# Spreading the layer zero modulation steps of a fused two-block transformer over every second weight block

## The chip, the cores and the metric

The kernel runs on one core of one Trainium2 chip. The metric is device time in microseconds (us). The kernel before takes 2114.54 us, the median of 3 runs (2113.99 to 2114.84).

The engines are called PE (TensorE), DVE (VectorE), ACT (ScalarE), POOL (GpSimd) and SP (SyncE, which issues the DMAs).

## The reference

Two stacks of two layers each run on 256 tokens of width 1024. The first stack is modulated by a condition vector `c`; only it matters here. Cut to what matters:

```python
c_act = jax.nn.silu(c)
for l in range(2):
    mod = c_act @ w_ada[l] + b_ada[l]                  # 6 x 1024 numbers
    sh1, sc1, gt1, sh2, sc2, gt2 = jnp.split(mod, 6, axis=-1)
    h = modulate(rms_norm(x, norm_mix[l]), sh1, sc1)
    p = h @ w_in[l]
    y_att  = dilated_mixture_attention(...)            # from p
    y_rwkv = rwkv7_time_mix(...)                       # from p, a scan over the tokens
    y_gmlp = chunked_spatial_gating(...)               # from p
    ys = jnp.stack([y_att, y_rwkv, y_gmlp], axis=2)
    gates = jax.nn.sigmoid(p[..., i2:])
    merged = jnp.sum(gates * (ys @ w_branch[l]), axis=2)
    x = x + gt1 * (merged @ w_out[l])
    h = modulate(rms_norm(x, norm_ffn[l]), sh2, sc2)
    x = x + gt2 * conv_gated_ffn(h, ...)
```

The second stack (`second_block`: gated feed-forward, windowed attention beside a convolution, feed-forward, a per-layer embedding) needs no modulation.

## The kernel before

Activations stay on chip, features on the partitions. All large weights come as one stream of 664 blocks of eight 128 x 128 tiles (512 KB a block), in the order in which PE uses them. A block is loaded into one of seven buffers `raw`, ACT rounds it into one of five buffers `hi`, and DVE subtracts (`lo = raw - hi`, line 214 in the profile). PE then multiplies with both halves for accuracy.

The modulation is computed beside this, on DVE alone: for each of the 48 columns of 128 numbers of a layer, a 128 x 1024 block of `w_ada` is loaded into one of two buffers `ada` (512 KB by DMA) and one DVE instruction multiplies it with the row `crow` and sums (line 231). It is followed by a short read of the accumulator into `mod`. This pair is called a modulation step. Sixteen of layer 0's are done at the start of the program; the other 32, and then the 48 of layer 1, are spread through what follows.

What sets the order is `ORDER`, a list that `main_order` writes out by hand and that each of the five engines' programs walks through, and a `Flow` object in each of them. `Flow.tiles(n)` counts weight tiles; after each block (8 tiles) it calls the block's own work and then `tick`, which advances every side chain by one step: the recurrent scan (`rwkv`), attention, and `ada`, the modulation. On DVE the block's own work at the end of block b is the `lo` of block b+4. On ACT it is the `hi` of block b+5, and on SP the load of block b+7. SP's side step is the load of the `ada` block two further on, which waits until DVE has done the modulation step of this tick, since it takes over its buffer. All DMAs of SP are issued in the order of its program.

How often `ada` takes a step:

```python
def ada_order(f, step):
    for l in range(L):
        for m in range(0 if l else FIRST, 48):
            while f.pause:
                yield
            step(l, m)
            if m % 8 == 7:
                f.mods.add((l, m // 8))
            yield
            if l or m >= 40:
                yield
            if f.slow:
                yield
```

So a layer 0 column below 40 takes a step at every block unless `slow` is set, and the rest at every second block, or every third under `slow`. `("pause", ...)` items stop it; `("pause if", (l, 4))` stops it only if group 4 (columns 32 to 39) of that layer is already done; `("need", l, g)` catches up at once if group g is not.

The items of a layer, with the blocks of layer 0 (layer 1's are 148 further on): the `z` projections and `gmlp` (up to block 26, modulation paused), `gate`, `qk`, `v`, `branch2` (to 46), `gate` again (to 54), `branch0`, `branch1` and `merge` (54 to 70), `wout` (70 to 78), `norm2` (to 80), `up` (80 to 124), `down` (124 to 146). Names used later: `var_t` and `rs_t` hold the two gates in turn that `branch0` multiplies; `mg` holds the merged branches in two halves, made by the four `merge` items on ACT (high half) and DVE (low half), and read by PE in `wout`; `xT` is the residual stream, which DVE updates after each of the eight `wout` results, and whose squares PE sums in `norm2` before the second norm; `pfh` and `pfl` are operands of a small projection (`p_proj`) that PE does around `norm2`.

In `wout` the first two results are summed together, over k from 0 to 7, so PE needs the last quarter of `mg` (k = 6, 7) 12 tiles after its start.

Of the kernel before, what the change touches and what calls it, by code (L numbers as in the profile page):

```python
# [375 lines left out]
def main_order():  # L376

    s = []
    for l in range(L):
        s += [("start1", l), ("z first", l)] if l else [("pause", True), ("start",)]  # L380
        for p in (6, 2, 3, 0, 1, 4, 5):
            s += [("z", l, p), ("flag", ("z", l, p))]
            if p == (3 if l else 0):
                s += [("rwkv", l), ("pause", True)]
        if l == 0:
            s += [("bias table",)]
        s += [("gmlp v", l), ("token norm", l), ("gmlp u", l, 0), ("gmlp u", l, 1), ("gate", l, 2, 0),
              ("until", ("ln", l)), ("spatial", l), ("gate", l, 2, 1), ("gmlp y", l), ("flag", ("gmlp", l)),
              ("pause", False), ("gate", l, 2, 2), ("gate", l, 2, 3), ("until", ("prep", l))]
        s += [("qk", l, p) for p in range(4)] + [("v", l), ("attention1", l)]  # L390
        s += [("branch2", l, p) for p in range(4)] + [("flag", ("ys free", l)), ("until", ("qk free", l))]
        s += [("gate", l, 1, p) for p in range(4)] + [("finish", ("att1", l))]
        s += [("branch0", l, 0), ("branch0", l, 1), ("branch0", l, 2), ("finish", ("rwkv", l)), ("pause if", (l, 4))]
        s += [("branch0", l, 3), ("pause if", (l, 4)), ("branch1", l, 0), ("merge", l, 0), ("branch0", l, 4), ("branch1", l, 1), ("branch0", l, 5),
              ("merge", l, 1), ("branch0", l, 6), ("branch1", l, 2), ("branch0", l, 7), ("merge", l, 2), ("branch1", l, 3)]
        s += [("need", l, 2), ("out half", l), ("merge", l, 3), ("pause if", (l, 4))]
        s += [("wout", l, p) for p in range(4)] + [("need", l, 3), ("need", l, 4), ("norm2", l), ("slow", True)]
        s += [("up first", l)] + [("up", l, m) for m in range(KF + 2)] + [("down", l, p) for p in range(4)]
    for l in range(L):
        s += [("f first", 1, l)] + [("f", 1, l, m) for m in range(KF + 2)] + [("f down", 1, l, p) for p in range(4)]  # L400
        s += [("mixer2", l), ("c", l, 0), ("c", l, 1), ("c", l, 2), ("conv2", l), ("c", l, 3), ("c last", l)]
        s += [("qkv", l, 0), ("qkv", l, 1), ("taps", l, 0), ("qkv", l, 2), ("v2", l), ("taps", l, 2), ("qk norm", l), ("attention2", l)]
        s += [("gate2", l, 0), ("v2 turn", l)] + [("gate2", l, p) for p in range(1, 8)] + [("gate2 last", l), ("finish", ("att2", l))]
        s += [("attn out", l, 0), ("attn out", l, 1), ("attn out", l, 2), ("finish", ("conv2", l)), ("conv out", l, 0),
              ("attn out", l, 3), ("conv out", l, 1), ("conv out", l, 2), ("conv out", l, 3)] + [("wo", l, p) for p in range(4)]
        s += [("f first", 2, l)] + [("f", 2, l, m) for m in range(KF + 2)] + [("f down", 2, l, p) for p in range(4)]
        s += [("ple", l, m) for m in range(8)]
    return s


ORDER = main_order()
MAIN, WIDE, GEN, ONE, STAT = (0, 1, 3), (0, 1, 4, 5, 6, 7), (4, 5, 6, 7), (2,), (3,)
CONV, ATT2 = (4,), (5, 6, 7, 2)
# [2620 lines left out]
```

How the kernel before makes its waits and increments, by code:

```python
    def wait_ge(self, sig, name=None):  # L190
        if name is None:
            v = sig.n
        else:
            assert self.e is None or name in sig.at, name
            v = sig.at.get(name, 0)
        if v > self.seen.get(id(sig), 0):
            self.seen[id(sig)] = v
            if self.e is not None:
                self.e.wait_ge(sig.handle, v)
# [429 lines left out]
            def take(pool, use):  # L629
                before = ps.take(pool, use)
                if before in ps.freed:
                    pe.wait_ge(*ps.freed[before])
                return ps(use)
# [3 lines left out]
            def tile(keys):  # L637
                b, i = divmod(f.n, BT)
                n = len(keys)
                assert i + n <= BT
                if e is None:
                    order.extend(keys)
                pe.wait_ge(v_main, ("lo", b))
                f.n += n
                cols = slice(i * 128, (i + n) * 128)
                return hi[b % HL][:, cols], lo[b % RAW][:, cols], [("block", b)] if i + n == BT else []
# [1 line left out]
            def plain_tile(key):  # L649
                b, i = divmod(f.n, BT)
                if e is None:
                    order.append(key)
                pe.wait_ge(d_raw[b % RAW], ("raw", b))
                f.n += 1
                return raw[b % RAW][:, i * 128:(i + 1) * 128], [("block", b)] if i == BT - 1 else []
# [17 lines left out]
            def h_in(norm):  # L674
                return (lambda k: t256(hh, k), lambda k: t256(hl, k), lambda k: pe.wait_ge(v_main, ("h", norm, k)))
```

## Time and profile before

| | |
|---|---|
| median of the runs | 2114.54 us |
| profiled execution, own time | 2114.51 us |
| span of its trace | 2112.7 us |
| PE busy | 2091.4 us, 99% |
| PE weight load busy | 1900.4 us, 90% |
| DVE busy | 1641.4 us, 78% |
| ACT busy | 1232.7 us, 58% |
| DMA queue of SP | 422.08 MB, 59.2% of 16 engines |

Busy shares are over the whole span. Matmuls are pipelined: a row gives a matmul of 256 columns some 0.28 us, while the next starts 0.12 us after it. The span is 1.8 us short of the execution's own time, which agrees with the median.

### The profile page before, as it was taken

What the parts mean: (1) busy time and instruction counts of PE and PEld (TensorE: products, weight loads), DVE (VectorE), ACT (ScalarE), POOL (GpSimd) and SP (SyncE); (2) the same over time, 40 slices, a digit from 0 to 9 for tenths busy, and PEclk for the clock granted to TensorE, in tenths of its full rate; (3) what the DMA queues carried; (4) which work ended last, traced back from release to release, by engine and by line L of the source; (5) the groups of instructions that cost most, each with busy time, mean ns of one, the idle gap of its engine ahead of it and who ended that gap; (6) DMA issues with size and microseconds to landing.
All of it is one profiled execution on the core that took longest, in us unless ns stands there. A gap on an engine that the chain in (4) does not pass through costs nothing.

```text
span 2112.7 us, 39171 instructions
## 1 busy us (share of the span) xinstructions
PE 2091.4 (99%) x16342; PEld 1900.4 (90%) x16342; DVE 1641.4 (78%) x2528; ACT 1232.7 (58%) x1999; POOL 13.1 (1%) x20
## 2 busy tenths in 40 slices
PE   8999999999999999999999999999999999999999
PEld 6888999999998899998888989888898888998888
DVE  7899788888887788877887657787688765788876
ACT  4754756555755656555665448665475644766554
POOL 0000000000000000000000000000000000000000
PEclk9999999999999999999999999999999999999999
DMA  9566567768644467655555654555555557356553
GB/s 372 199 212 211 178 218 256 244 225 289 225 157 170 165 210 235 212 187 189 184 191 187 231 159 155 203 190 189 189 181 189 190 196 221 134 178 208 190 189 131
DMA packets 122115, 424.59 MB, mean 201 GB/s; under 512 B 13465, under 2 KB 22041, under 8 KB 121170
## 3 DMA queue, kind: packets, MB, share of 16 engines
q1 hardware_dynamic: 121938, 422.08, 59.2%
q8 instruction: 129, 2.11, 0.4%
q14 instruction: 48, 0.39, 0.1%
HBM read 417.68 MB, written 4.35 MB: 200 GB/s over the span
## 4 chain that ended last, share of the span: by engine, by line
PE 88%; DVE 6%; ACT 4%; DMA 1%; issue 1%; POOL 0%; SPq 0%; ACTq 0%; DVEq 0%
PE bank L208 88%; ACT arena L259 2%; DVE arena L214 2%; DVE lo L214 2%; ACT hi L259 1%; DVE arena L222 1%; DMA raw<-W 1%; PE bank L211 0%; DVE sml L234 0%; DVE ada L231 0%; DMA xT<-x 0%; ACT L251 0%; DVE arena L218 0%; ACT L259 0%; DVE arena L237 0%
## 5 line engine op out<-in xcount | busy, mean ns | idle before, releaser
L208 PE MATMUL bank<-h,hi 128*128 128x256 f32 (+1 forms) x5248 | 1183.1, 312 | 0.0
L259 ACT ACTIVATE hi<-raw 128x1024 fp32r<-128x1024 f32 x656 | 689.1, 1057 | 530.8 <-PE bank L208 458.6
L208 PE MATMUL bank<-h,lo 128*128 128x256 f32 x3328 | 949.1, 285 | 1.4 <-ACT arena L259 1.2
L208 PEld LDWEIGHTS bank<-h,hi 128*128 128x128 f32 x5248 | 861.4, 190 | 60.3 <-issue 1.9
L214 DVE TENSOR_TENSOR lo<-raw,hi 128x1024 fp32r<-128x1024 f32 x656 | 791.8, 1220 | 96.0 <-ACT hi L259 95.1
L208 PEld LDWEIGHTS bank<-h,lo 128*128 128x128 f32 x3328 | 633.7, 190 | 13.3 <-issue 7.8
L208 PE MATMUL bank<-act,hi 128*128 128x512 f32 x1056 | 370.0, 393 | 0.0
L208 PE MATMUL bank<-act,lo 128*128 128x256 f32 x1056 | 294.7, 279 | 0.0
L208 PEld LDWEIGHTS bank<-act,hi 128*128 128x128 f32 x1056 | 197.9, 187 | 47.1
L208 PEld LDWEIGHTS bank<-act,lo 128*128 128x128 f32 x1056 | 197.9, 187 | 0.0
L259 ACT ACTIVATE arena<-arena 128x256 f32<-128x256 f32 (+4 forms) x202 | 98.5, 493 | 159.2 <-DVE arena L214 151.4
L259 ACT ACTIVATE arena<-bank 128x256 f32<-128x256 f32 (+3 forms) x419 | 170.5, 449 | 23.5 <-PE bank L208 22.0
L208 PE MATMUL bank<-arena 64*64 64x64 f32 (+8 forms) x2940 | 144.7, 281 | 5.0 <-DVE arena L222 2.2
L214 DVE TENSOR_TENSOR arena<-arena 128x256 f32<-128x256 f32 (+2 forms) x237 | 123.8, 527 | 22.0 <-ACT arena L259 17.9
L208 PEld LDWEIGHTS bank<-arena 64*64 64x64 f32 (+4 forms) x2940 | 105.9, 137 | 35.0 <-DVE arena L222 4.0
L214 DVE TENSOR_TENSOR act<-arena,act 128x256 fp32r<-128x256 f32 x132 | 56.0, 424 | 79.1 <-ACT act L259 78.6
L231 DVE CUSTOM_DVE_ANT_0 ada<-ada,crow,par 128x1024 f32<-128x1024 f32 x80 | 104.3, 1303 | 0.2
L222 DVE SCALAR_TENSOR_TENSOR arena<-arena,par 128x256 f32<-128x256 f32 (+1 forms) x124 | 60.5, 503 | 23.8 <-ACT arena L259 20.6
L214 DVE TENSOR_TENSOR arena<-bank,arena 128x256 f32<-128x256 f32 (+2 forms) x182 | 69.3, 424 | 3.4 <-ACT arena L259 3.4
L222 DVE SCALAR_TENSOR_TENSOR xT<-bank,xT 128x256 f32<-128x256 f32 x96 | 40.6, 422 | 35.1 <-PE bank L208 33.5
L259 ACT ACTIVATE act<-arena 128x256 fp32r<-128x256 f32 x132 | 52.9, 401 | 4.8 <-DVE arena L214 4.8
L208 PE MATMUL bank<-ysh,lo 128*128 128x256 f32 x192 | 55.0, 287 | 0.0
(153 smaller groups left out, 1943.6 us busy)
## 6 DMA issues: line engine op xcount, KB each, us to landing
raw<-W SPq DMA_DIRECT2D x664, 512.0 KB, 3.4
ada<-WA SPq DMA_DIRECT2D x80, 512.0 KB, 3.9
arena<-WA SPq DMA_DIRECT2D x16, 512.0 KB, 14.2
arena<-conv_rows SPq DMA_DIRECT2D x16, 280.0 KB, 5.9
arena<-taps SPq DMA_DIRECT2D x2, 1792.0 KB, 8.4
p_projected<-arena SPq DMA_DIRECT2D x2, 1024.0 KB, 7.6
arena<-p_projected SPq DMA_DIRECT2D x2, 1024.0 KB, 4.8
arena<-scr SPq DMA_DIRECT2D x10, 128.0 KB, 4.5
```

The costliest lines, as they stand in the source:

```text
L208: return self.done(lambda e: e.matmul(out, l, r, start=start, stop=stop, skip_group_check=True))
L214: return self.done(lambda e: e.tensor_tensor(out, a, b, op))
L222: return self.done(lambda e: e.scalar_tensor_tensor(out=out, in0=a, scalar=s, in1=b, op0=o0, op1=o1))
L231: return self.done(lambda e: e.tensor_tensor_reduce(out, a, b, 1.0, start, MUL, ADD, total))
L259: return self.done(lambda e: e.activation(out, in_, f, scale=scale, **kw))
```

## The change

One item is added to layer 0's list. `("slow", True)` stands right behind `("pause", False)`, after `gmlp y`. Layer 1's list is unchanged.

```diff
         s += [("gmlp v", l), ("token norm", l), ("gmlp u", l, 0), ("gmlp u", l, 1), ("gate", l, 2, 0),
               ("until", ("ln", l)), ("spatial", l), ("gate", l, 2, 1), ("gmlp y", l), ("flag", ("gmlp", l)),
-              ("pause", False), ("gate", l, 2, 2), ("gate", l, 2, 3), ("until", ("prep", l))]
+              ("pause", False)] + [("slow", True)] * (1 - l) + [("gate", l, 2, 2), ("gate", l, 2, 3), ("until", ("prep", l))]
```

`slow` is set back at layer 1's start, as before. Counting blocks through `ORDER` gives where the steps stand (number of blocks finished when the step is taken):

| | before | now |
|---|---|---|
| layer 0, blocks 27 to 50 | 24 steps, one at every block | 12 steps, one at every second |
| layer 0, 51 to 57 | 4 steps | 4 steps |
| layer 0, 59 to 69 (`branch0`, `merge`) | none | 6 steps |
| layer 0, 71 to 78 (`wout`) | none | 4 steps: 71, 73, 75, 78 |
| layer 0, `norm2` to `down` (79 to 145) | 23 steps, every third block | 22 steps, every third block, shifted (81 to 144) |
| layer 1, 147 to 207 | 21 steps | 21 steps |
| layer 1, 209 to 217 (`branch1`, `merge`) | none | 5 steps |
| layer 1, `up` | 8 steps, to 248 | 6 steps, to 242 |

The reason for the new places: in layer 0, group 4 was complete at block 50, and both `pause if` items at blocks 58 and 70 stopped the chain. Now it is complete at block 73. In layer 1 it was complete at 207 and is now at 213.

PE's, ACT's and POOL's instructions keep their order. DVE's and SP's change. In the order of DVE's instructions the numbers of buffers are kept (`lo_61` to `lo_67` are the seven buffers, so one row is one block).

DVE in the branch stage of layer 0, around blocks 63 to 65, as the difference of the order (`arena<-arena,bank` is the gated branch of a `branch1`, the rows on `var_t` are a `branch0`):

```order
 L214 TENSOR_TENSOR lo_64<-raw_52,hi_57 128x1024
+L231 ISA ada_68,mod<-ada_68,crow,par 128x1024
+L231 ISA mod 128x1
 L222 SCALAR_TENSOR_TENSOR arena<-arena,bank 128x512
 L214 TENSOR_TENSOR arena<-arena 128x512
 L214 TENSOR_TENSOR lo_65<-raw_53,hi_58 128x1024
 L214 TENSOR_TENSOR lo_66<-raw_54,hi_59 128x1024
+L231 ISA ada_69,mod<-ada_69,crow,par 128x1024
+L231 ISA mod 128x1
 L222 SCALAR_TENSOR_TENSOR var_t<-var_t,bank 128x256
 L214 TENSOR_TENSOR arena<-arena,var_t 128x256
```

A step is put in behind every second `lo`, ahead of the branch arithmetic of that block. Six of them stand in this stage.

DVE at the end of layer 0's `wout`, where the last result (`xT`, two instructions) is added and the gain of the second norm (`sml<-mod,par`) is formed:

```order
 L214 TENSOR_TENSOR lo_65<-raw_53,hi_57 128x1024
+L231 ISA ada_69,mod<-ada_69,crow,par 128x1024
+L231 ISA mod 128x1
 L222 SCALAR_TENSOR_TENSOR xT<-bank,sml,xT 128x256 x2
 L222 SCALAR_TENSOR_TENSOR sml<-mod,par 128x8
```

The step of block 78 stands between the last `lo` and the last update of `xT`. The step that stood inside the norm (block 79) is gone.

## Rows read from the trace of the kernel before

**Rows 1.** The page's part 1, busy time and instructions of each engine

```profile
PE 2091.4 (99%) x16342; PEld 1900.4 (90%) x16342; DVE 1641.4 (78%) x2528; ACT 1232.7 (58%) x1999; POOL 13.1 (1%) x20
```

**Rows 2.** Part 5: groups, busy us, mean ns, idle before; then part 6, issues

```profile
L214 DVE TENSOR_TENSOR lo<-raw,hi 128x1024 fp32r<-128x1024 f32 x656 | 791.8, 1220 | 96.0 <-ACT hi L259 95.1
...
L231 DVE CUSTOM_DVE_ANT_0 ada<-ada,crow,par 128x1024 f32<-128x1024 f32 x80 | 104.3, 1303 | 0.2
...
raw<-W SPq DMA_DIRECT2D x664, 512.0 KB, 3.4
```

**Rows 3.** Waits of PE, 128 to 160, 190 to 194, 194 to 200 us

```profile
PE bank L208 <- ACT arena L259: 0.3, 1, 0.3
...
PE bank L208 <- DVE arena L222: 1.4, 2, 1.1
...
PE bank L208 <- DVE arena L222: 0.2, 1, 0.2
```

**Rows 4.** Chain that ended last: start us, us, what; both layers' scans

```profile
189.29 1.19 DVE ada L231
...
193.63 5.33 PE bank L208 x72
...
221.54 1.46 PE bank L211 x12
...
682.50 5.33 PE bank L208 x72
...
710.41 1.46 PE bank L211 x12
```

**Rows 5.** Windows: stretch, its us, busy us by engine, PEclk, DMA, GB/s

```profile
260.00:292.00 32.00, 32.00 (x269) 32.00 (x269) 27.66 (x39) 17.20 (x24) 0.00 (x0) 1.00 0.60 208
292.00:315.00 23.00, 23.00 (x134) 20.07 (x134) 20.55 (x35) 13.23 (x18) 0.00 (x0) 1.00 0.62 201
```

**Rows 6.** Timeline of DVE, layer 0 branches: start, us, instruction, idle before

```profile
262.19 1.28 DVE L231 CUSTOM_DVE_ANT_0 ada<-ada,crow,par 128x1024 f32<-128x1024 f32 x1
263.40 0.08 DVE L231 DVE_READ_ACCUMULATOR2_ANT mod<- 128x1 f32 x1
...
269.71 0.42 DVE L222 SCALAR_TENSOR_TENSOR var_t<-var_t,bank 128x256 f32<-128x256 f32 x1 [1.25 <-ACT var_t L259]
...
291.28 0.42 DVE L222 SCALAR_TENSOR_TENSOR var_t<-var_t,bank 128x256 f32<-128x256 f32 x1 [1.92 <-ACT var_t L259]
...
296.00 0.69 DVE L214 TENSOR_TENSOR mg<-arena,mg 128x512 fp32r<-128x512 f32 x1 [0.69 <-ACT mg L259]
```

**Rows 7.** Timeline of PE in layer 0's `wout`

```profile
296.40 0.28 PE L208 MATMUL bank<-mg,lo 128*128 128x256 f32 x1
...
296.74 0.39 PE L208 MATMUL bank<-mg,lo 128*128 128x256 f32 x1
```

**Rows 8.** Timeline, `wout` and `norm2` of layer 0, DVE, PE and ACT

```profile
298.30 1.23 DVE L214 TENSOR_TENSOR lo<-raw,hi 128x1024 fp32r<-128x1024 f32 x1 [0.47 <-ACT hi L259]
...
316.00 1.00 DVE L222 SCALAR_TENSOR_TENSOR xT<-bank,sml,xT 128x256 f32<-128x256 f32 x2
...
316.48 1.73 PE L208 MATMUL bank<-arena,cst 128*128 128x256 f32 x6
...
317.04 0.42 ACT L259 ACTIVATE arena<-xT 128x256 f32<-128x256 f32 x1 [0.67 <-DVE xT L222]
```

**Rows 9.** Timeline of DVE, layer 1's branches

```profile
771.52 0.42 DVE L222 SCALAR_TENSOR_TENSOR var_t<-var_t,bank 128x256 f32<-128x256 f32 x1 [0.75 <-ACT var_t L259]
...
774.83 0.42 DVE L222 SCALAR_TENSOR_TENSOR rs_t<-rs_t,bank 128x256 f32<-128x256 f32 x1 [0.69 <-ACT rs_t L259]
...
777.29 0.69 DVE L222 SCALAR_TENSOR_TENSOR arena<-arena,bank 128x512 f32<-128x512 f32 x1 [0.45 <-PE bank L208]
...
783.03 0.42 DVE L222 SCALAR_TENSOR_TENSOR var_t<-var_t,bank 128x256 f32<-128x256 f32 x1 [1.92 <-ACT var_t L259]
...
787.74 0.69 DVE L214 TENSOR_TENSOR mg<-arena,mg 128x512 fp32r<-128x512 f32 x1 [0.69 <-ACT mg L259]
```

## The prediction

> **What bounds the kernel now.** I read the busy times first. PE is busy for 99% of the span and DVE for 78% [rows 1]. So PE looks like the bound, and a change that only moves DVE work can act in one way alone: where PE waits for DVE, or would come to. The work itself does not change: 80 modulation steps before and after, and 656 `lo` of some 1.2 us each, one a block [rows 2]. A step keeps DVE for 1.21 us: it starts at 262.19, and the accumulator read, with the next instruction beside it, starts at 263.40 [rows 6].
>
> Next, the waits of PE in the stage that is relieved, blocks 27 to 50 or 120 to 225 us. DVE is nearly full there, and one might take it for the bound. But PE's waits add up to little: 0.3 us for ACT before 160 us, 1.4 us for DVE near 192 us in two waits, and 0.2 us in 194 to 200 [rows 3]. From 200 to 260 us the same view has one more of 0.2 us, near 200, which is the same wait cut by the window.
>
> The chain shows why. Shortly before 193.63 it runs through DVE, modulation steps included. Then it is on PE. And it can be compared with layer 1, which takes a step only at every second block already. The same scan work lasts from 193.63 to 221.54 in layer 0 and from 682.50 to 710.41 in layer 1: 27.91 us in both [rows 4]. In these 28 us a step at every block costs PE nothing against one at every second.
>
> Last, the stage that receives the steps. In `branch0`, `branch1` and `merge` of layer 0 (260 to 292 us) PE is busy for all of the 32 us and DVE for 27.66; in `wout` (292 to 315 us) DVE is busy for 20.55 of 23 [rows 5]. So there is idle time of 4.3 and 2.5 us. What counts is where it lies, and what hangs on DVE's last instruction of each stage.
>
> **The change part by part.**
>
> 1. *Twelve steps leave blocks 27 to 50.* That is 12 x 1.21 = 14.5 us of DVE time. What PE can gain is bounded by its waits, 0.3 + 1.4 + 0.2 = 1.9 us [rows 3]. One of the two waits near 192 and the small ones also occur in stretches of layer 1 at the slower rate. I take 1.4 us, of the bounds 0 and 1.9: the steps at blocks 40, 42 and 44 go, which frees 3.6 us just before the largest wait.
>
> 2. *Six steps enter layer 0's branch stage (blocks 59 to 69).* 6 x 1.21 = 7.3 us. DVE waits there for the gates from ACT, 1.25 us at 269.71 and 1.92 us at 291.28, and these waits absorb steps [rows 6]; the first takes in one step of 1.21, the last 1.92. The other idle times, of some 0.7 us before an `mg`, are answers of ACT to DVE's own result (0.69 at 296.00), so they move with it. Thus the low half of the last `mg` comes 7.3 - 1.2 - 1.9 = 4.1 us later, where all else holds. PE needs it at once: it is written from 296.00 to 296.69, and the matmul that reads it starts at 296.74, where a row of this form lasts 0.39 us in place of 0.28, so PE has already waited 0.1 us [rows 6, 7]. Nothing covers this: `wout` is PE's next work and its other k are done. Cost 4.1 us, with bounds 0 and 7.3 (six steps, nothing absorbed). The `lo` blocks run ahead, so they stay covered: the wait of PE would begin only if DVE lagged by more than about three blocks.
>
> 3. *Four steps enter `wout` (71, 73, 75, 78).* 4 x 1.21 = 4.8 us. The 4.1 us of part 2 moved PE and DVE alike, so this counts anew. One idle time of 0.47 us absorbs [rows 8]. From `pfl` at 302.35 us on DVE works without a break to the last `xT` at 316.00, and PE is just in time again: it starts the sums of squares at 316.48, and the last of their operands is the square that ACT forms from 317.04 to 317.46, while six matmul records fill 316.48 to 317.85 [rows 8]. All of the norm follows behind. So PE gets 4.8 - 0.5 = 4.3 us more to wait, 4.4 with rounding on the side of the `pfl` chain, which goes through ACT. Bounds 1.2 (the step of block 78 alone, which stands between the last `lo` and the last `xT`) and 4.8. The step in the norm at block 79 goes, but PE has the rest of `p_proj` to do meanwhile, and I count nothing for it.
>
> 4. *Five steps enter layer 1's branch stage (209 to 217), none its `wout`.* 5 x 1.21 = 6.0 us. DVE idles more there behind the first of them: 0.75, 0.69, 0.45 and 1.92 us [rows 9], 3.8 us in all. The last `mg` at 787.74 is as tight for PE as in layer 0. Cost 6.0 - 3.8 = 2.2 us, bounds 0 and 6.0.
>
> 5. *The steps in `up` and `down` shift by one block or two, and layer 1's `up` loses two.* No wait of PE stands there. Counted at nothing; the cover is that PE's `lo` are three blocks ahead, and if that were gone one step would cost 1.2 us.
>
> 6. *SP.* The 512 KB loads move with the steps. SP waits with a load until the step of the same tick is done, and weights queue behind it. A weight block lands 3.4 us after its issue [rows 2], and is issued seven blocks of 2.9 us ahead, so a delay of some 6 us is still covered. Counted at nothing, bounds 0 and one block, 2.9 us.
>
> Sum: -1.4 + 4.1 + 4.4 + 2.2 = +9.3 us. The profiled execution took 2114.51 us itself (span 2112.7 and 1.8 around it), which is the median of the runs (2114.54) within 0.03. So 2114.5 + 9.3 = 2123.8 us.
>
> A rule stands against this sum. The Trainium skill, in Perfetto Trace Analysis, "Identifying the Most-Contended Engine", says that the engine with the highest occupancy is the most contended one, that DVE's occupancy can be read as its distance from roofline, and that for TensorE the share of weight loads is to be read in place of matmul time. By that, DVE with 78% has room, PE with weight loads of 90% decides, and steps moved on DVE would change nothing: 2114.5. The rule's mechanism here is the first rival.
>
> **The rivals.**
>
> *No change, from 2110.3 to 2118.7.* DVE's lag is taken up by slack that I don't see. For it: PE shows no wait in 260 to 330 us, and DVE had 4.3 us of idle time in a stage that gets 7.3. Against it: the two places where PE is within 0.1 us of DVE [rows 7, 8]. It needs the `mg` chain of both layers to be hidden; then the norm's 4.4 less 1.4 gives 2117.5.
>
> *Faster.* The relieved stage gives more than its waits show, since DVE there runs late by a block and more, and the late stages absorb the steps. The mechanism: twelve steps less let PE start each matrix step of the scan earlier, at up to 1.21 us each. It decides if more than 9.3 us of the 14.5 came back, or if parts 2 to 4 are covered. At full cover of those and the whole of rows 3 it gives 2114.5 - 1.9 = 2112.6, so to pass 2110.3 it needs over 4 us from the scan. The equal 27.91 us of both layers speaks against it [rows 4].
>
> *Much slower, over 2127.* The loads decide. The weights behind a step's load are late, ACT rounds late, and DVE waits for ACT on top of its own lag: about one block, 2.9 us, in layer 0's branch stage, so 2126.7, and more if `wout` has it too.
>
> **How the numbers follow.** The forecast, with at least two of parts 2 to 4 at about their size, has 0.74. No change 0.12, much slower 0.10, faster 0.04. A measurement here tells 0.2%, or 4.2 us, from no change. So faster has 0.04, same 0.12, and slower the rest, 0.84. The range goes from 2117.0 (the norm alone, a little hidden) to 2127.5 (parts 2 to 4 and one late block).
>
> **What the profile after would show.** If part 2 is right, DVE has no idle time before the `var_t` that stood at 291.28, and PE waits some 4 us in the first two blocks of layer 0's `wout`, for `mg` (L214, from DVE). If part 3 is, PE waits 4 us more right behind `wout`, for the squares of `xT`, on ACT or DVE. If part 4 is, a wait of 2 us stands at the same place of layer 1, and none at its norm beyond what was there. If part 1 is, the wait near 192 us shrinks from 1.4 to some 0.3 us, and the blocks around it last the same. The forecast is wrong if PE's waits for DVE in `wout` are under 1 us, if the stretch from 120 to 225 us gets shorter by over 3 us, or if waits for raw weights show up.

## The result and the profile after

| | before | after |
|---|---|---|
| median of the runs | 2114.55 us (4 runs, 2113.99 to 2114.84) | 2125.69 us (4 runs, 2123.51 to 2126.32) |
| profiled execution, own time | 2114.51 us | 2126.32 us |
| span of its trace | 2112.7 us | 2124.2 us |

After divided by before is 1.0051, 95% interval [1.0038, 1.0063]. The forecast was 2123.8 us in a range of 2117.0 to 2127.5. So the kernel became slower by 11.1 us where 9.3 were forecast.

First the busy times of the page after, part 1 and one group of part 5, which answer to [rows 1, 2]:

```profile
PE 2096.0 (99%) x16342; PEld 1904.0 (90%) x16342; DVE 1641.0 (77%) x2528; ACT 1232.7 (58%) x1999; POOL 13.1 (1%) x20
...
L231 DVE CUSTOM_DVE_ANT_0 ada<-ada,crow,par 128x1024 f32<-128x1024 f32 x80 | 103.5, 1294 | 0.1
```

DVE did the same work in the same time; only its place is new. PE is "busy" for 4.6 us more with the same 16342 matmuls. That is a first sign of something besides waits: some matmuls got slower.

Next, PE's waits in the stretches of the prediction: 190 to 194, 260 to 300, 300 to 340 and 700 to 850 us (engine, what waited, releaser: us in all, times, longest). The trace of before has 1.4 us near 192 [rows 3], and PE was busy for all of 260 to 315 us [rows 5].

```profile
PE bank L208 <- DVE arena L222: 0.2, 1, 0.2
...
PE bank L208 <- DVE var_t L222: 2.7, 1, 2.7
PE bank L208 <- DVE mg L214: 0.9, 1, 0.9
...
PE bank L208 <- ACT arena L259: 2.6, 1, 2.6
PE bank L208 <- DVE arena L214: 1.4, 1, 1.4
...
PE bank L208 <- DVE mg L214: 0.9, 1, 0.9
PE bank L208 <- DVE var_t L222: 0.4, 1, 0.4
```

The wait near 192 is gone but for 0.2 us. Layer 0's `wout` begins with 3.6 us of waits, its norm has 4.0, layer 1's `wout` 1.3. All are for the chains that the prediction named, though 2.7 us of them end at `var_t` and not at `mg`.

To price a stage, waits are not enough, since they leave out slower matmuls. So I took the start of the last `lo` matmul of each weight block as the end of that block, counted from the first instruction of the trace, in both traces, and subtracted: what each stage became longer by, in us. Stages in blocks; 26 to 60 holds the relieved stage, 60 to 75 the end of the branches with the start of `wout`, 75 to 90 the end of `wout`, the norm and the start of `up`, 205 to 222 the end of layer 1's branches and the start of its `wout`, 222 to 235 its norm.

| kernel | to 26 | 26-60 | 60-75 | 75-90 | 90-205 | 205-222 | 222-235 | 235 on | all |
|---|---|---|---|---|---|---|---|---|---|
| forecast | 0 | -1.4 | +4.1 | +4.4 | 0 | +2.2 | 0 | 0 | +9.3 |
| after | -0.24 | -1.24 | +4.00 | **+6.95** | +0.26 | +1.72 | 0.00 | +0.04 | +11.49 |

One trace against one trace: blocks up to 26, which no kernel here changes, differ by -0.4 to +0.3 us from trace to trace in all the kernels below, and 90 to 205 by -0.1 to +0.7. One column of after is off by far more than that: 75 to 90. Within it, 5.59 us fall to block 78 and 1.36 to block 79.

What stands there, from DVE's timeline after (start, us, instruction). The three rows answer to 316.00 of [rows 8], where the `lo` stood directly ahead of the last `xT`:

```profile
320.44 1.22 DVE L214 TENSOR_TENSOR lo<-raw,hi 128x1024 fp32r<-128x1024 f32 x1
321.57 1.28 DVE L231 CUSTOM_DVE_ANT_0 ada<-ada,crow,par 128x1024 f32<-128x1024 f32 x1
...
322.78 1.00 DVE L222 SCALAR_TENSOR_TENSOR xT<-bank,sml,xT 128x256 f32<-128x256 f32 x2
```

ACT and PE behind it, against 317.04 and 316.48 of [rows 8]:

```profile
320.58 1.13 PE L208 MATMUL bank<-arena,cst 128*128 128x256 f32 x4 [1.42 <-DVE arena L214]
...
323.81 0.42 ACT L259 ACTIVATE arena<-xT 128x256 f32<-128x256 f32 x1 [2.22 <-DVE xT L222]
...
324.28 1.22 PE L208 MATMUL bank<-arena,cst 128*128 128x256 f32 x2 [2.58 <-ACT arena L259]
...
325.51 0.41 PE L208 MATMUL bank<-pfh,hi 128*128 128x256 f32 x1
325.73 0.41 PE L208 MATMUL bank<-pfl,hi 128*128 128x256 f32 x1
...
330.39 0.28 PE L208 MATMUL bank<-pfh,lo 128*128 128x256 f32 x1
```

PE waits 1.42 and 2.58 us, 4.0 in all, where 4.4 were forecast. But then its matmuls of 256 columns take 0.41 us and start 0.22 apart; at 330.39 they are back at 0.28. The windows say why (stretch, its us, busy us of PE, weight loads, DVE, ACT, POOL with counts, granted clock, DMA share, GB/s):

```profile
320.00:322.00 2.00, 1.13 (x4) 0.68 (x4) 2.00 (x4) 1.37 (x2) 0.00 (x0) 1.00 0.65 264
322.00:324.00 2.00, 0.00 (x0) 0.00 (x0) 1.82 (x5) 0.19 (x1) 0.16 (x3) 0.88 0.14 29
324.00:326.00 2.00, 1.72 (x6) 1.54 (x7) 0.00 (x0) 0.69 (x2) 0.01 (x1) 0.50 0.72 246
326.00:328.00 2.00, 2.00 (x11) 2.00 (x11) 1.26 (x3) 1.34 (x4) 0.00 (x0) 0.50 0.04 8
328.00:330.00 2.00, 2.00 (x12) 2.00 (x11) 2.00 (x6) 1.18 (x3) 0.00 (x0) 0.50 0.48 104
330.00:332.00 2.00, 2.00 (x17) 2.00 (x17) 2.00 (x5) 1.19 (x2) 0.00 (x0) 0.92 0.40 158
```

The granted clock falls in the wait, from 1.00 (2.4 GHz) to 0.50 (1.2 GHz), and stays there until some 330 us. In before the same twelve microseconds have 1.00 throughout and 19 matmuls in each 2 us; here it is 11 and 12. One of those windows of before:

```profile
324.00:326.00 2.00, 2.00 (x19) 2.00 (x18) 2.00 (x5) 0.04 (x1) 0.00 (x0) 1.00 0.00 0
```

The page's own row of clocks shows 9 in all 40 slices: a slice is 53 us, so a fall of 7 us is invisible on it. It does show in the mean clock of a whole execution, and not in the profiled one alone: 0.997 to 0.998 in all four of after, 0.999 to 1.000 in all of before. The Trainium skill (TensorE: Matmul & The Clock Gate, "HAM oscillation") says that waits of PE for data can throttle it again, so that the next work starts cold; this trace agrees, with 0.50 behind one pair of waits.

### The profile page after: what moved, and what is told of

It is laid out like the page before. It is cut to its first block, busy times and chain, and to the rows that moved or that the text cites. A ratio compares the mean times of both kernels' runs of the same rounds, so it can differ in the third digit from the quotient of the medians.

```text
span 2124.2 us, 39171 instructions
## 1 busy us (share of the span) xinstructions
PE 2096.0 (99%) x16342; PEld 1904.0 (90%) x16342; DVE 1641.0 (77%) x2528; ACT 1232.7 (58%) x1999; POOL 13.1 (1%) x20
## 4 chain that ended last, share of the span: by engine, by line
PE 84%; DVE 8%; ACT 4%; DMA 2%; issue 1%; SPq 0%; ACTq 0%; DVEq 0%
PE bank L208 84%; DVE lo L214 3%; ACT arena L259 2%; DVE arena L214 2%; DMA raw<-W 2%; ACT hi L259 1%; DVE arena L222 1%; DVE ada L231 1%; PE bank L211 0%; DVE sml L234 0%; DVE xT L222 0%; DVE mg L214 0%; DMA xT<-x 0%; ACT L259 0%; ACT L251 0%
## 5 line engine op out<-in xcount | busy, mean ns | idle before, releaser
L259 ACT ACTIVATE arena<-xT 128x256 f32<-128x256 f32 (+1 forms) x90 | 37.9, 421 | 29.8 <-DVE xT L222 27.2
```

The costliest lines, as they stand in the source:

```text
L259: return self.done(lambda e: e.activation(out, in_, f, scale=scale, **kw))
```

## The experiments

All were timed beside the kernel before. "Trace" is the block table above made for each kernel. First all results, then each. In the edits shown, `SHORT` and `LATE` stand for the lists of steps that the kernels write out, and the semaphore calls at the ends of lines are left out.

| kernel | median us (range, runs) | ratio to before, 95% |
|---|---|---|
| e1 all late steps short | 2115.20 (2114.55 to 2115.74, 10) | 1.0002 [0.9993, 1.0012] |
| e2 those in `wout` short | 2119.15 (2117.74 to 2120.61, 10) | 1.0022 [1.0012, 1.0031] |
| e3 those in layer 0's branches short | 2121.36 (2120.93 to 2123.01, 6) | 1.0033 [1.0021, 1.0045] |
| e4 PE kept busy in the norm's waits | 2123.21 (2122.84 to 2123.32, 4) | 1.0041 [1.0026, 1.0056] |
| e5 half rate in `v` and `attention1` only | 2114.26 (2113.25 to 2115.99, 11) | 0.9998 [0.9989, 1.0007] |
| e6 one more instruction ahead of the last `xT` | 2116.85 (2116.24 to 2117.41, 11) | 1.0010 [1.0001, 1.0019] |
| e7 the same ahead of a `var_t` | 2115.04 (2113.96 to 2115.71, 11) | 1.0001 [0.9993, 1.0010] |
| e8 late loads tiny | 2125.05 (2123.41 to 2126.00, 4) | 1.0048 [1.0034, 1.0062] |
| e9 only the last `wout` step short | 2121.77 (2120.85 to 2124.06, 5) | 1.0035 [1.0023, 1.0047] |
| e10 PE kept busy in both waits | 2123.02 (2122.22 to 2123.39, 5) | 1.0039 [1.0025, 1.0053] |
| e11 half rate in `v` only, same count | 2114.09 (2113.22 to 2114.84, 11) | 0.9997 [0.9989, 1.0006] |

| trace | to 26 | 26-60 | 60-75 | 75-90 | 90-205 | 205-222 | 222-235 | 235 on | all |
|---|---|---|---|---|---|---|---|---|---|
| e1 | -0.29 | -1.25 | +1.09 | +0.43 | +0.28 | +0.02 | 0.00 | +0.05 | +0.33 |
| e2 | -0.24 | -1.25 | +3.94 | +0.85 | +0.18 | +0.46 | 0.00 | +0.67 | +4.60 |
| e3 | -0.08 | -1.25 | +0.43 | +6.40 | +0.14 | +1.11 | 0.00 | +0.06 | +6.80 |
| e4 | -0.35 | -1.27 | +4.34 | +3.85 | +0.53 | +1.25 | -0.01 | +0.03 | +8.38 |
| e5 | -0.08 | -1.26 | +0.01 | -0.01 | -0.09 | +0.78 | +0.39 | +0.02 | -0.25 |
| e6 | -0.16 | +0.01 | +0.02 | +1.12 | -0.05 | 0.00 | +1.11 | +0.02 | +2.07 |
| e7 | +0.28 | -0.01 | +0.02 | -0.01 | -0.14 | +0.02 | -0.01 | +0.01 | +0.17 |
| e8 | -0.35 | -1.25 | +3.94 | +6.84 | +0.65 | +0.99 | 0.00 | +0.03 | +10.85 |
| e9 | -0.43 | -1.26 | +5.87 | +1.56 | +0.39 | +0.02 | 0.00 | +0.01 | +6.16 |
| e10 | -0.38 | -1.28 | +4.09 | +4.25 | -0.01 | +0.76 | 0.00 | +0.13 | +7.56 |
| e11 | -0.29 | -1.27 | +0.38 | 0.00 | +0.04 | +0.02 | 0.00 | +0.01 | -1.11 |

The 0.67 us of e2 behind block 235 are one wait of PE for a DMA near 1225 us, 0.57 us, which no other trace has.

### Is it the steps' time on DVE (e1, e2, e3)?

On the kernel after, the steps that stand late work on 8 columns instead of 1024; e1 has all fifteen of them in the set, e2 the four of layer 0's `wout`, e3 the six of its branch stage.

```diff
-                v.ttr(src, src, crow, P("b_ada", l, m), mod[:, at:at + 1])
+                w = 8 if (l, m) in SHORT else 1024
+                v.ttr(src[:, 0:w], src[:, 0:w], crow[:, 0:w], P("b_ada", l, m), mod[:, at:at + 1])
```

> The changed kernel, but the fifteen modulation steps that came new into the branch stages and the `wout` of layer 0 and the branch stage of layer 1 multiply 8 columns in place of 1024. The rest of these products is left out; loads, waits and order are kept. DVE theory (late DVE work moves `mg` and the last `xT`, and TensorE's clock falls behind the long wait): all of the loss goes and the gain of part 1 stays, 2113.2 us. Rival, loads (weights stand behind the loads of modulation in SP's queue): the loads are still there, so most of the 11 us stays, over 2120 us. Rival, the clock falls for another reason: 2116 us.

Measured 2115.2, 10.5 us below after. Fifteen instructions, some 18 us of DVE in all, carry nearly the whole loss. The theory of the loads (over 2120) falls. That of DVE was 2 us too low; what is left over stands in the trace in three places, 1.09, 0.43 and 0.28 us (for the first see e8).

> The changed kernel, with only the four steps in layer 0's `wout` (blocks 71, 73, 75, 78) cut to 8 columns; the rest of these four products is left out. DVE theory: the wait behind `wout` (1.4 + 2.6 us in the trace) and the stretch at the lower clock behind it both go, together the 7.0 us that blocks 78 and 79 lost: 2125.7 - 7.0 = 2118.7 us. If the clock fell for another reason than this wait, only 4.4 us go: 2121.3. Loads theory: 2125.7.

> The changed kernel, with only the six steps in layer 0's branch stage (blocks 59 to 69) cut to 8 columns; the rest of these six products is left out. DVE theory: the 4.0 us that blocks 70 and 71 lost go, and the wait behind `wout` stays as it is since PE and DVE were moved alike: 2121.7 us, with the lower clock still there. Rival, the lag of the branch stage is carried on into `wout`: then up to 4 us more go behind `wout` too, 2117.7. Loads theory: 2125.7.

e2 gave 2119.15, e3 2121.36, both within 0.5 us of DVE's account. Each half of the change costs its part without the other. e3 also shows the odd column: at the start of its `wout` PE waits 0.3 us alone, yet 75 to 90 is 6.40 longer. Its waits of PE in 260 to 340 us, then two windows of its trace:

```profile
PE bank L208 <- ACT arena L259: 2.6, 1, 2.6
PE bank L208 <- DVE arena L214: 1.4, 1, 1.4
PE bank L208 <- DVE mg L214: 0.3, 1, 0.3
```

```profile
320.00:322.00 2.00, 1.13 (x3) 0.95 (x4) 0.44 (x2) 0.42 (x1) 0.17 (x3) 0.50 0.77 231
322.00:324.00 2.00, 2.00 (x11) 2.00 (x10) 0.88 (x2) 1.23 (x3) 0.00 (x0) 0.50 0.09 35
```

The same 4.0 us of waits as in after, the same clock of 0.50 behind them. e2, with 0.8 us of wait there, keeps 1.00 and loses 0.85.

### Is the rest the clock (e4, e10, e9)?

e4 adds nine matmuls without use to PE's program of after, in the two waits of the norm:

```diff
+                    if norm == ("n2", 0) and m in ("sum", parts[-1]):
+                        for _ in range(3 if m == "sum" else 6):
+                            pe.mm(adab[:, 0:256], C("ones"), C("cos"), True, True)
```

> The changed kernel, with nine more matmuls of 256 columns in PE's waits behind layer 0's `wout` (three before the first sum of squares, six before the last), whose results nobody reads. DVE theory with the clock as a consequence of PE's wait: the waits are as long (4.0 us) but PE is not idle, the granted clock stays at 1.0 in the next 8 us, and the 2.5 us that the lower clock took come back: 2123.2 us. Rival, the fillers stand in PE's way (nine records of some 0.43 us each against waits of 4.0): 2125.7 or up to 1 us more. Rival, the clock falls whatever PE does: 2125.7 to 2126.7.

Measured 2123.21, as the theory of the clock said: 2.5 us less with nine matmuls more. The column fell from 6.95 to 3.85. The window of the trace of e4:

```profile
318.00:330.00 12.00, 12.00 (x81) 11.00 (x80) 9.57 (x20) 6.50 (x13) 0.17 (x3) 1.00 0.53 185
```

1.00 where after has 0.50. But the same trace shows the clock low in another place, behind the 2.6 us wait at the merge:

```profile
292.00:294.00 2.00, 0.00 (x0) 0.00 (x0) 2.00 (x4) 0.58 (x1) 0.00 (x0) 1.00 0.93 346
294.00:298.00 4.00, 3.92 (x14) 3.40 (x15) 3.55 (x7) 0.91 (x2) 0.00 (x0) 0.57 0.83 314
```

After has 1.00 there, with 13 matmuls in 296 to 298 us. So one wait of this length lowers the clock in one execution and not in another. I took it for another 2 us to be had, and e10 adds fillers there too:

```diff
+                if (l, p) == (0, 0):
+                    for _ in range(6):
+                        pe.mm(adab[:, 0:256], C("ones"), C("cos"), True, True)
```

> The kernel with fillers behind `wout`, and six more filler matmuls ahead of layer 0's `wout`, where PE waited 2.6 us for the bank that the last `var_t` frees and where the clock fell in that kernel's trace (0.57 in 294 to 298 us). Clock theory: no stretch below 1.0 is left, and the 1.7 us go that 4 us at 0.57 cost: 2123.2 - 1.7 = 2121.5 us. Rival, the clock falls at one of the two places in every run, whatever PE does: 2123.2. Rival, the fillers take as much as they give: 2123.2 to 2124.

Measured 2123.02, where 2121.5 was expected, a miss: no gain over e4 that could be told (0.2 us). The clock did as wanted, here and in the norm, where 318 to 330 us have 1.00 as in e4:

```profile
292.00:300.00 8.00, 6.94 (x37) 5.58 (x36) 7.24 (x12) 4.68 (x7) 0.00 (x0) 1.00 0.87 311
```

So a clock restored at the merge gained nothing that shows. The chain of waits of the kernel after says why. Here a few of its pieces in 286 to 330 us (start, us, what); the pieces left out are two more steps, `lo`, `xT`, `pfl` and branch work of DVE and two pieces of ACT of 0.6 us each:

```profile
292.68 1.20 DVE ada L231
293.88 0.34 DVE var_t L222
...
298.51 0.69 DVE mg L214
...
300.33 1.20 DVE ada L231
...
321.66 1.20 DVE ada L231
...
323.81 0.43 ACT arena L259
...
324.28 5.92 PE bank L208 x24
```

From 286 to 324 us DVE sets the end, not PE. A slow PE in between only shortens its own next wait. In e4 the trace has 4.34 and 3.85 in the two columns, in e10 4.09 and 4.25: what the fillers gave at the merge, the norm's wait took back. That the six fillers got in PE's way by as much as the clock gave is the other reading; no run separates the two. But the last `mg` of DVE came 3.93 us late in e4 and 4.08 in e10, against PE at block 60, and PE can't be sooner than that: the column 60 to 75 has 4.34 and 4.09. At 324.28 the chain goes over to PE, and there a low clock costs in full.

e9 makes only the last step of `wout` (block 78) short, `SHORT` being `(0, 41)` alone.

> The changed kernel, with only the step of block 78 cut to 8 columns (the rest of this product is left out), the one that stands between the last `lo` and the last `xT`. DVE theory: PE's last wait, for the square of that `xT`, shrinks by some 1.1 us, from 2.6 to 1.5: 2124.4 us if the clock falls as before, and 2122 if the shorter wait does not lower the clock. Rival, this place costs nothing by itself: 2125.5.

Measured 2121.77, near the second figure, 2122. The wait for ACT is 1.5 us and the clock behind it stays at 1.00. In this trace too it fell at the merge instead, where a wait of 2.9 us stood:

```profile
294.00:296.00 2.00, 1.70 (x6) 1.50 (x7) 1.97 (x4) 0.82 (x1) 0.00 (x0) 0.50 0.66 207
296.00:298.00 2.00, 2.00 (x8) 1.71 (x8) 1.81 (x4) 0.20 (x1) 0.00 (x0) 0.50 0.97 391
```

Its columns are 5.87 and 1.56, where after has 4.00 and 6.95. The sum is 3.5 us less: 1.2 for the step, the rest the clock where PE sets the end. The medians differ by 3.9, but that is not the same 3.5: the whole traces differ by 5.3 us, of which 1.7 lie in layer 1 (column 205 to 222), where this edit changes nothing. So the median near 2122 does not weigh the clock; the two columns and the windows do.

### One instruction in two places (e6, e7)

On the kernel before, one reduction of 128x1024 on DVE in each layer, 1.13 us each, with no load and no other step moved. e6 has it ahead of the last `lo` of `wout`, e7 in the branches ahead of the `var_t` that waits 1.92 us for ACT.

```diff
+                    if c in (81, 229):        # e7: (72, 220)
+                        v.reduce(sml[:, 255:256], raw[c % RAW][:, :], ADD)
```

> The kernel before with one DVE instruction more (a sum over a raw block, 1.1 us, whose result nobody reads) ahead of the `lo` that stands before the last `xT` of `wout`, in both layers. DVE theory: PE is just in time for the squares there, so layer 0 pays the full 1.1 us, and layer 1, where DVE waited 0.3 us for PE before that `xT`, some 0.8: 2114.8 + 1.9 = 2116.7 us, the clock at 1.0. Rival, slack: 2114.8.

> The kernel before with the same extra DVE instruction (1.1 us, result not read) ahead of the second `lo` before the last `var_t` of the branch stages, where DVE waits 1.92 us for ACT, in both layers. DVE theory: the wait absorbs it, 2114.8 us. Rival, each DVE instruction in these stages costs its time wherever it stands: 2117.0.

e6 measured 2116.85, e7 2115.04. The trace is sharper: 1.12 and 1.11 us in the two norms for e6, and for e7 no column behind block 26 is off by more than 0.14. PE's waits in e6, at 260 to 340 and 750 to 840 us:

```profile
PE bank L208 <- ACT arena L259: 1.1, 1, 1.1
...
PE bank L208 <- ACT arena L259: 0.9, 1, 0.9
```

And the `var_t` of e7, whose idle time was 1.92 us [rows 6]:

```profile
291.56 0.42 DVE L222 SCALAR_TENSOR_TENSOR var_t<-var_t,bank 128x256 f32<-128x256 f32 x1 [0.78 <-ACT var_t L259]
```

1.14 us of idle time were used up, and nothing behind it moved. Both halves of the method of parts 2 and 3 hold: idle time of DVE behind ACT absorbs, the stretch before the last `xT` passes everything on.

### Do the loads cost anything (e8)?

On the kernel after, the loads of the same fifteen steps carry 8 columns, 4 KB, instead of 512 KB. The steps read old data and last as long as before.

```diff
-                    s.dma(rada[b % RAWA][:, :], T["WA"][b])
+                    w = 8 if divmod(b - RAWA, 48) in LATE else CB
+                    s.dma(rada[b % RAWA][:, 0:w], T["WA"][b][:, 0:w])
```

> The changed kernel, where the loads that SP issues behind the fifteen late steps fetch 8 columns in place of 1024 (the products of the steps that use them are therefore of other data); DVE's work and SP's waits are kept. DVE theory: nothing changes, 2125.7 us. Rival, the traffic of the moved loads delays the weights (ACT waited for raw blocks in the branch stage in the trace with short steps): up to 1 us faster, 2124.7. Rival, loads decide: under 2120.

Measured 2125.05, 0.6 us under after, inside both ranges. Yet something happened with the weights. ACT's waits for them, before (262 to 298 us) and after (262 to 296 us):

```profile
ACT hi L259 <- DMA raw<-W: 5.6, 2, 4.5
```

```profile
ACT hi L259 <- DMA raw<-W: 16.4, 8, 4.7
```

SP holds a load until the step that frees its buffer is done, and the weights stand behind it in the same queue. SP's waits for steps, before and after (240 to 300 us):

```profile
SPq L205 <- DVE mod L231: 8.9, 2, 7.8
```

```profile
SPq L205 <- DVE mod L231: 32.2, 8, 7.8
```

ACT waits 10.8 us longer, in 8 waits instead of 2; the longest, near 267 us, stood in before too. In e8, where SP is held as long (32.3 us) and only the bytes are gone, ACT waits 10.6 us. So of the 10.8 us some 5.8 are the traffic of the loads and 5.0 their place in the queue. In layer 0 this costs nothing: DVE, which needs ACT's `hi`, was later still. The columns 60 to 90 of e8 are within 0.11 us of after's, though ACT waits 5.8 us less. For the place in the queue, which e8 leaves as it is, the chain speaks: behind the wait near 267 us, which before has as well, it holds no piece of a DMA up to the norm.

In layer 1 it is different. Four steps stand between the first and the last `mg`, 4.8 us. DVE's timeline after, with both `mg` and the one idle time between them that is not an answer to its own result:

```profile
772.82 0.69 DVE L214 TENSOR_TENSOR mg<-arena,mg 128x512 fp32r<-128x512 f32 x1 [0.70 <-ACT mg L259]
...
786.56 0.42 DVE L222 SCALAR_TENSOR_TENSOR rs_t<-rs_t,bank 128x256 f32<-128x256 f32 x1 [1.45 <-ACT rs_t L259]
...
799.21 0.69 DVE L214 TENSOR_TENSOR mg<-arena,mg 128x512 fp32r<-128x512 f32 x1 [0.68 <-ACT mg L259]
```

And ACT's, just before that `rs_t`:

```profile
785.20 1.06 ACT L259 ACTIVATE hi<-raw 128x1024 fp32r<-128x1024 f32 x1 [3.45 <-DMA raw<-W]
786.16 0.37 ACT L259 ACTIVATE rs_t<-bank 128x256 f32<-128x256 f32 x1
```

The weights are 3.45 us late, ACT's `rs_t` stands behind them in order, and DVE idles 1.45 us for it. From `mg` to `mg` DVE needs 26.39 us in after; in before the same stretch, to the 787.74 of [rows 9], is 24.31, and in e2, e3, e8, e9 and e10 it is 24.84 to 24.92. So where no weights come too late for DVE the four steps lengthen it by 0.5 to 0.6 us, and here the late block adds 1.5. It is not the only trace with such a block: e4 has 25.82, with DVE idle for 0.88 us behind ACT's `hi`, and e5 25.19, with 0.24. In this stretch ACT waits 9.8 us for weights in after, 7.4 in e3, where DVE does not idle for it, and not at all in e9, whose loads are the full ones. What decides this the runs do not show.

The column 205 to 222 is 1.72 in after, 0.99 in e8 and 0.02 in e9. It is the sum of two things: the growth of this stretch (2.1, 0.5 and 0.6 us) and where its first `mg` stands against PE, 0.3 us early in after, 0.5 late in e8, 0.6 early in e9, measured as the shift of this `mg` less the shift of PE at block 205. So the late block costs after 1.5 us of DVE's time, but its column is only 0.7 above that of e8. The 0.6 us between the medians of e8 and after are of that size, but the ranges overlap.

In e1, where DVE is early again and ACT still waits 14.5 us in layer 0, the cover there is gone too. The chain of its trace runs through such weights, and behind them through ACT's `rs_t` to DVE (start, us, what):

```profile
276.72 6.91 DMA raw<-W
...
284.61 0.38 ACT rs_t L259
```

I take the 1.09 us of its column 60 to 75 for that; the chain agrees, but no run separates it.

### A version that beats both (e5, e11)?

e5, on the kernel before, sets `slow` ahead of `v` and takes it back behind the fourth `branch2`, to have part 1's gain alone.

```diff
-        s += [("qk", l, p) for p in range(4)] + [("v", l), ("attention1", l)]
+        s += [("qk", l, p) for p in range(4)] + [("slow", True)] * (1 - l) + [("v", l), ("attention1", l)]
```

> The kernel before with `slow` on only from `v` to `branch2` of layer 0 (blocks 38 to 46): the steps at blocks 39, 41, 43 and 45 move to 51 to 55, where the trace of before shows DVE idle, group 4 is complete at block 54, and both pause items stop the chain as before. DVE theory: the 1.3 us that block 44 gained in the changed kernel stays, and nothing else moves, 2114.8 - 1.3 = 2113.5 us. Rival, the gain is an artefact of one profile and does not show in the median (the kernel with the fifteen short steps came out at 2115.2, where 2113.2 was expected): 2114.8. Rival, the denser steps at 51 to 55 delay `branch0`: up to 2 us slower, 2116.

The gain is in the trace, -1.26, and so is a price. Two steps fewer are done by block 57, so group 4 of layer 1 is not complete at block 207, nothing stops the modulation there, and five steps stand in its branches, at the blocks 209 to 217 as in after. With layer 0's branches and `wout` as in before, 0.78 and 0.39 us come back there. Median 2114.26, where 2113.5 was expected. e11 takes `slow` back two items earlier and lets the half rate begin at `m >= 44` instead of 40, so that no step is left over.

> The kernel with `slow` in `v` only, mended: `slow` ends two pairs earlier and the columns 40 to 43 are taken one a block too, so that layer 0 is as far at block 58 as in the kernel before and no step is left over for layer 1's branch stage (in the trace of the version without this, blocks 219 and 226 gave back 1.1 of the 1.3 us gained at block 44). DVE theory: 2114.7 - 1.3 = 2113.4 us. Rival, the denser steps at 45 to 58 delay layer 0's branches: 2114.7 or more.

The trace has -1.27, nothing in layer 1, and +0.38 in layer 0's branches, where the steps now stand denser; it is -1.11 in all, 0.3 of it in blocks that the edit doesn't change. Median 2114.09, 0.7 below before, interval [0.9989, 1.0006]. It is the lowest of all kernels here, but not separable from before, and 2113.4 was expected.

## Why the prediction was right, and where not, point by point

**What bounds the kernel: right.** PE at 99% with the end set by DVE in a few tens of microseconds. The rule of the Trainium skill (Perfetto Trace Analysis, "Identifying the Most-Contended Engine"), by which 2114.5 would have stood, doesn't agree with the measured 2125.7: DVE was the emptier engine on the whole and the full one in two stages.

**Part 1, -1.4: right.** -1.24 to -1.28 in all ten traces that have it, all of it at block 44, e5 and e11 with little else among them. The medians of e5 and e11 (0.5 and 0.7 us under before) can't confirm a figure of this size.

**Part 2, +4.1: right in size, incomplete in the mechanism.** 4.00. DVE's idle time before the second `var_t` is gone, as foreseen, and the idle time at the first is 0.16 us where it was 1.25:

```profile
268.36 0.42 DVE L222 SCALAR_TENSOR_TENSOR var_t<-var_t,bank 128x256 f32<-128x256 f32 x1 [0.16 <-ACT var_t L259]
...
293.80 0.41 DVE L222 SCALAR_TENSOR_TENSOR var_t<-var_t,bank 128x256 f32<-128x256 f32 x1
```

But 2.7 of the 3.6 us of waits are not for the last `mg`. They end at this last `var_t`, which reads the bank that PE wants next. I had only asked when PE's operands come, not when its banks come free. The sum was the same since both stand on one chain of DVE.

**Part 3, +4.4: this is the term that was mis-sized, 6.95 measured.** The lateness of the last `xT` was right: 1.42 + 2.58 = 4.0 us of waits, 4.25 us in e10's column. The missing 2.7 us (6.95 less 4.25) are TensorE's clock at 0.50 behind that wait, which no term and no bound of the part held; its upper bound, 4.8, was too low for it. Nine filler matmuls gave back 2.5 of it by the medians (e4).

**Part 4, +2.2: right in size, for the wrong reason.** 1.72, seen as waits of 0.4 for `var_t` and 0.9 for `mg`. But DVE's idle time absorbed more than the 3.8 us that I had added up: its stretch grows by only 0.5 to 0.6 us with four steps where the weights are in time, and the five cost 0.02 in e9. The late weights added 1.5 us to the stretch in the trace after. Over the kernels whose five steps are whole the column is 0.02 to 1.72, with 0.78 in e5, where layer 0's late stages are as before. That the trace after lies near 2.2 is luck.

**Part 5, 0: right within 0.3 us** (column 90 to 205), though e4 and e8 have 0.53 and 0.65 there. All of it falls to block 154, where a wait of PE for DVE (`arena`), 0.2 us at 535 us in before, is 0.5 in after and 0.8 in e8.

**Part 6, 0: wrong in the mechanism.** I counted a delay of 6 us as covered. Weights did come late, 16.4 us of waits on ACT in layer 0, where before has 5.6, and 9.8 in layer 1. The prediction named this as a sign against itself, and it is there. In layer 0 DVE was later than ACT; in layer 1 it was not, in one place, and that cost DVE 1.5 us, inside the part's bounds of 0 and 2.9.

**The rivals.** No change: refuted, nothing of the `mg` chain was hidden. Faster: refuted, the scan gave 1.24 us of the 9.3 needed. Much slower through loads: e1, which keeps all loads and SP's waits for the steps (31.5 us in 240 to 300 us) and is 0.6 us above before, refutes it as the main cause, and e8 for the bytes alone, at 0.6 us of 11.1; its chain (weights late, ACT late, DVE waits for ACT) is real, but in layer 1 and at half the price. Still, the time came out closer to its figure, 2126.7, than the mechanism deserved: 2.7 us of clock stood in for its 2.9 us of late block.

**Still open:** whether the late weights are all of e1's 1.09 us, what decides if weights come late in layer 1, and what decides at which of two waits the clock falls.

## What to carry to other kernels

Price a moved instruction where it lands: the idle time of its own engine behind others absorbs it, the stretch before a result on which the whole next stage hangs passes it on in full. Where a wait of several microseconds is new on TensorE, look at the granted clock behind it in windows of 2 us, and count the slower matmuls only if PE sets the end there. Follow a moved load through its queue too: what stands behind it comes late when its buffer is released late.

## What the runs showed of the hardware that I had not expected

- Waits of 1.42 and 2.58 us with 1.1 us of matmuls between them brought TensorE from 1.00 to 0.50 for some 7 us (323 to 330 us), in after, e3 and e8. A single wait of 2.6 to 2.9 us did it in e4 (for 3.4 us) and e9, not with 2.7 us in after or 2.6 us in e2 and e8. Waits of 1.5 us (e9) and 0.8 us (e2) in the norm did not.
- Nine matmuls of 256 columns in the norm's waits held 1.00, and the kernel with more work was 2.5 us faster.
- Of SP's queue: loads held back by their buffers, with the weights behind them, raised ACT's waits for weights in layer 0 from 5.6 us in two to 16.4 us in eight. Tiny loads in the same places left 10.6 us. In layer 1 the longest such wait was 3.5 us in after, and e9's trace had none.
- At 0.50 the matmul of 256 columns takes 0.41 us in a row where it takes 0.28 at 1.00, and starts 0.22 us after the last one where it was 0.12.
